# A shorter head of expert dots ahead of the second block's first half: HEAD from 26 to 12

## The reference, cut to what matters

```python
a = gelu(einsum('tpkd,td->tpk', u[idx], t))          # 128 rows of u per token
y = einsum('tpk,tpkd->td', g * a, v[idx])            # 128 rows of v per token
x = x + gt2 * y;  x = rms_norm(x, norm_f)            # end of the first block
# second block, layer 0: short convolution + memory attention, out projection, SwiGLU
# second block, layer 1: windowed attention + memory attention, out projection, SwiGLU
```

## Time and profile before

| | us |
|---|---|
| median of 3 runs | 2847.36 (2844.52 to 2847.91) |
| the profiled execution's own time | 2847.91 |
| its span | 2845.8 |
| PE busy | 2320.9 (82%) |
| DVE busy | 1931.0 (68%) |
| POOL busy | 1064.3 (37%) |
| ACT busy | 961.0 (34%) |

### The profile page before, as it was taken

How to read it: one execution, slowest core, us unless ns; L and a number is a source line. 1 busy time by engine, 2 the same in 40 slices (tenths; PEclk the granted TensorE clock), 3 DMA queues, 4 the chain that set the end, 5 groups by cost and what they waited for, 6 DMA issues and landing times.

```text
span 2845.8 us, 43889 instructions
## 1 busy us (share of the span) xinstructions
PE 2320.9 (82%) x16542; PEld 1721.4 (60%) x16542; DVE 1931.0 (68%) x4242; ACT 961.0 (34%) x1655; POOL 1064.3 (37%) x1029
## 2 busy tenths in 40 slices
PE   7998987989355555665759989869999899999998
PEld 4776776746101111111648777626788899986998
DVE  3454766799866667767997777664545676665765
ACT  4454655221100000001324333324333554455544
POOL 0000000446677777776565766576551000000000
PEclk7999999999698988988869999979999999999999
DMA  7331102879999999999989999999997345551554
GB/s 306 118 142 62 55 23 83 338 295 401 409 409 409 409 409 409 409 409 392 341 312 361 408 408 409 408 353 406 376 408 287 133 164 189 188 179 61 178 192 141
DMA packets 225234, 810.35 MB, mean 285 GB/s; under 512 B 24704, under 2 KB 30720, under 8 KB 223232
## 3 DMA queue, kind: packets, MB, share of 16 engines
q0 software_dynamic: 147456, 536.94, 48.3%
q1 hardware_dynamic: 77568, 270.61, 26.3%
HBM read 805.35 MB, written 2.10 MB: 284 GB/s over the span
## 4 chain that ended last, share of the span: by engine, by line
PE 37%; DMA 22%; DVE 14%; issue 5%; POOL 3%; ACT 1%; SPq 0%; POOLq 0%; DVEq 0%; ACTq 0%
PE ps L1844 9%; PE ps L1845 9%; PE ps L1846 9%; DMA pe_ring<-in_v,pe_vidx 7%; DVE pe_ring L2675 6%; DMA pe_ring<-in_u,pe_idx 6%; PE ps L1784 5%; DMA pe_more<-in_u,pe_idx 3%; DVE la_w_lo L2723 3%; DMA pe_more<-in_v,pe_vidx 1%; DMA la_k<-in_v,pe_vidx 1%; POOL pe_ring L1677 1%; PE ps L1739 1%; PE ps L1923 1%; PE ps L665 1%
## 5 line engine op out<-in xcount | busy, mean ns | idle before, releaser
L1844 PE MATMUL ps<-la_h_hi,la_w_hi 128*128 128x256 f32 x1856 | 531.8, 287 | 32.7 <-DVE la_w_lo L2723 25.9
L1671 POOL DMA_INDIRECT pe_ring<-in_u,pe_idx x419 | 447.8, 1069 | 287.1 <-DVE pe_dots L2675 139.1
L1784 PE MATMUL ps<-pe_ring,pe_spot 128*32 128x512 f32 x1616 | 398.7, 714 | 182.5 <-DMA pe_ring<-in_v,pe_vidx 158.5
L1846 PE MATMUL ps<-la_h_hi,la_w_lo 128*128 128x256 f32 x1856 | 524.2, 282 | 0.0
L1845 PE MATMUL ps<-la_h_lo,la_w_hi 128*128 128x256 f32 x1856 | 524.1, 282 | 0.0
L2723 DVE TENSOR_TENSOR la_w_lo<-la_w_raw,la_w_hi 128x1024 fp32r<-128x1024 f32 (+1 forms) x368 | 440.0, 1196 | 77.4 <-ACT la_w_hi L2299 76.7
L2299 ACT ACTIVATE la_w_hi<-la_w_raw 128x1024 fp32r<-128x1024 f32 (+1 forms) x368 | 379.7, 1034 | 323.5 <-DMA la_w_raw<-in_down 97.2
L1677 POOL DMA_INDIRECT pe_ring<-in_v,pe_vidx x404 | 416.7, 1032 | 175.8 <-issue 104.0
L1844 PEld LDWEIGHTS ps<-la_h_hi,la_w_hi 128*128 128x128 f32 x1856 | 355.2, 191 | 67.6 <-DVE la_w_lo L2723 42.9
L2675 DVE CUSTOM_DVE_ANT_0 pe_ring<-pe_ring,ps 128x1024 f32<-128x1024 f32 x249 | 297.9, 1219 | 117.9 <-DMA pe_ring<-in_u,pe_idx 114.4
L1845 PEld LDWEIGHTS ps<-la_h_lo,la_w_hi 128*128 128x128 f32 x1856 | 352.6, 190 | 0.4
(11 more groups left out here) (392 smaller groups left out, 3817.4 us busy)
## 6 DMA issues: line engine op xcount, KB each, us to landing
la_w_raw<-in_gate SPq DMA_DIRECT2D x88, 512.0 KB, 4.2
la_w_raw<-in_up SPq DMA_DIRECT2D x88, 512.0 KB, 4.5
la_w_raw<-in_down SPq DMA_DIRECT2D x64, 448.0 KB, 3.8
la_w_raw<-in_a_in SPq DMA_DIRECT2D x40, 512.0 KB, 5.4
wring<-in_w_in SPq DMA_DIRECT2D x32, 512.0 KB, 3.8
la_w_raw<-in_down SPq DMA_DIRECT2D x32, 512.0 KB, 3.7
wring<-in_wq SPq DMA_DIRECT2D x22, 512.0 KB, 7.3
xT<-in_w_mod_rows SPq DMA_DIRECT2D x8, 1024.0 KB, 4.9
```

The lines of the kernel that those rows point to most:

```text
L1671: pool.indirect_dma_start(row(n), None, io["u"], bass.IndirectOffsetOnAxis(idx[:, t, j:j + 1], 0)).then_inc(land[GATHERS[n][0]], 16)
L1784: return pe.matmul(ps[PER * grp:PER * grp + PER, half, :], spot[:, j // TOKENS % 2, grp, lo:lo + PER], row(n)[:, half * 512:(half + 1) * 5 ...
L1844: pe.matmul(slot(n), parts_hi[:, n % SPLIT, i, :], hi[:, k, :], start=first, stop=False)
L1846: return pe.matmul(slot(n), w_lo[:, n % RAW, i, :], hi[:, k, :], start=False, stop=last)
```

## The change

`HEAD` goes from 26 to 12. In the head on DVE, eight dots between the third low part of weights and the wait for the norm go, and six after the last `chunk_lo`; the eight dots ahead of the low parts and the four between the `scale_x` stay (with other indices).

```diff
-    EARLY, HEAD, IN_PSUM = GROUPS_U * GROUP_U, 26, 8
+    EARLY, HEAD, IN_PSUM = GROUPS_U * GROUP_U, 12, 8
...
                     for u in range(SPLIT - 1):
                         split_lo(u)
-                    for j in range(EARLY + 8, EARLY + 16):
-                        dot(2, j)
                     dve.wait_ge(rooted, rooted_at(0, -1))
                     for k in range(KC):
                         scale_x(p, k)
                         if k:
                             chunk_lo(p, 0, k - 1, ROWS_B["norm_mix"])
                         if k % 2:
-                            dot(2, EARLY + 16 + k // 2)
+                            dot(2, EARLY + 8 + k // 2)
                     chunk_lo(p, 0, KC - 1, ROWS_B["norm_mix"])
-                    for j in range(EARLY + 20, EARLY + HEAD):
-                        dot(2, j)
```

## The result

The changed kernel took 2868.8 us (median of 4 runs, 2865.5 to 2873.0) beside 2847.6 for the kernel before (4 runs, 2844.5 to 2851.1): a ratio of 1.0082 [1.0067, 1.0095]. It is slower by 21 to 23 us where +9.0 was forecast, and lies above the forecast's range. The profiled execution took 2873.6 us for a span of 2871.5; its further 4 us beside the median arise behind `half(0)`, most of them in 2521 to 2721 us, and the medians don't show them.

A forecast was written before the change was run, and what follows sets the result against it. It took `half(0)` as a relay, paced by DVE, then DMA, then PE. Terms -2.4 (to tick 38) + 7.7 + 0 + 3.7 = +9.0 us on the median 2847.4 gave 2856.4 us; 8-in-10 range 2843 to 2864.

The forecast's parts named there:

- The head: Start of `half(0)`: eight dots ahead of the scaling go, so the first product comes 9.3 us earlier.
- The reload: First reload of a weight tile, for which DVE waits 3.47 us: saves 2.3 us (0 to 3.5).
- Out projection: Layer 0, ticks 30 to 38: seven more dots on a nearly full DVE, +6.9 us (+1.6 to +8.2).
- Feed-forward and q, k, v: Ticks 38 to 118: six more gather uses where DMA sets the pace, 1.28 us each, +7.7 us.
- Last stretch: Out projection and feed-forward, ticks 158 to 226: eight more rows of v at PE's 0.46 us, +3.7 us.
- Layer 1's attention (118 to 158): Ticks 118 to 158, pace called mixed: 74 gather uses instead of 75, 0 us (-1.3 to 0).
- Rival 3: Whole debt at the DMA's price, last stretch DMA-bound: +13.5 us, 2860.9 us, up to 2866; chance 0.16.
- Rival 1: Early start survives, buffers in flight lend the gathers: -8.9 us, 2838.5 us; chance 0.14.
- the marks named for a right forecast: Included: first product at 1366.6 us, DVE idle 9 us, attention 4 to 6 us later, last gather 8 later.
- the three named for a wrong one: Below 400 GB/s in 1540 to 1840 us with PE full; attention earlier; PE awaiting v rows in last feed-forward.
- The rule beside the rows: DVE dots reading two SBUF operands slow POOL's gather issue through a shared port, 0.94 to 1.97 us.
- The price named beside the forecast: Ticks 38 to 118, if POOL at 2.27 us a gather set the pace: 13.6 us, sum +14.9.

The follow-up runs named there:

- the repeat: The changed kernel run once more, nothing altered: 1.0072, 2871.9 us.
- LAG -9: Kernel before, old head, with every gather's use due 14 earlier: 0.9972, 2845.0 us beside 2850.5.
- units of 2.0 ticks: Kernel before with an attention unit counting 2.0 ticks instead of 2.5, so fewer gathers fall there: 0.9981, 2847.2 us beside 2852.9.
- changed, LAG -9: Changed kernel with every use 14 earlier, giving the due values of the kernel before: 0.9987, 2849.0 us beside 2851.2 for the kernel before.
- changed, paid by tick 24: Changed kernel with a clock that makes up the 14 owed uses by tick 24: 1.0008 against the kernel before, 2853.4 us.
- changed, paid by tick 118: Changed kernel with a clock that pays the 14 owed uses evenly by tick 118: 1.0025, 2857.9 us beside 2850.5 for the kernel before.
- HEAD 20: Kernel before without only the six head dots behind the last `chunk_lo` (six owed): 1.0016, 2855.7 us.
- LAG 12: Kernel before, old head, with uses due seven later by the due values alone: 1.0006, 2853.4 us beside 2850.5.
- HEAD 18: Kernel before without only the eight head dots ahead of `scale_x` (eight owed): 1.0026, 2859.3 us.
- LAG 19: Kernel before, old head, with every gather's use due 14 later: 1.0084, 2875.1 us beside 2851.2.

## Why the prediction was wrong

**What held.** The head: -8.8 measured, -9.3 forecast. The reload: the whole 3.5 us saved, forecast 2.3. Out projection: +9.6 between products 24 and 32, forecast +6.9; DVE's 53 instructions there instead of 42 take 30.66 us instead of 24.86, the stage grows from 30.3 to 39.9 us, and its PE clock falls from 1.00 to 0.87. At product 32 the kernel stood at -1.1, forecast -2.4. Feed-forward and q, k, v: +9.1, forecast +7.7, at 406 GB/s. Last stretch: +2.0 to +3.0, forecast +3.7, PE full as before. Up to product 108 the sum was off by 2.7 us.

**The step that failed** is "Layer 1's attention (118 to 158). 74 uses instead of 75: 0 (-1.3 to 0)". It measured +10.5 us: 145.2 instead of 134.7, and 145.6 in the repeat. The step counted uses in a stage called "mixed" and priced their number. The number was right: between the cuts 90 rows are used in both kernels (34 dots and 56 rows of v after, 30 and 60 before), and 92 gathers stand there where 90 stood. What it left out is what sets the stage's pace. POOL's groups in that stage of the changed kernel (number, busy time, mean ns | idle time before them and what ended it):

```profile
L1677 POOL DMA_INDIRECT pe_ring<-in_v,pe_vidx x62 | 63.2, 1019 | 26.0 <-issue 17.1 <-PE ps L1784 7.8 <-DVE pe_dots L2675 1.1
L1671 POOL DMA_INDIRECT pe_ring<-in_u,pe_idx x23 | 30.8, 1338 | 15.9 <-PE ps L1784 8.4 <-issue 6.4 <-DVE pe_dots L2675 1.1
L1677 POOL DMA_INDIRECT pe_htok<-in_v,pe_vidx x4 | 3.7, 937 | 1.2 <-issue 1.2
L1671 POOL DMA_INDIRECT pe_htok<-in_u,pe_idx x3 | 3.7, 1249 | 0.9 <-issue 0.9
```

The same of the kernel before:

```profile
L1677 POOL DMA_INDIRECT pe_ring<-in_v,pe_vidx x63 | 65.8, 1045 | 19.3 <-issue 18.0 <-PE ps L1784 1.2
L1671 POOL DMA_INDIRECT pe_ring<-in_u,pe_idx x20 | 24.7, 1233 | 16.7 <-PE ps L1784 11.2 <-issue 5.5
L1677 POOL DMA_INDIRECT pe_htok<-in_v,pe_vidx x4 | 4.2, 1044 | 3.9 <-PE ps L1784 3.0 <-issue 0.9
L1671 POOL DMA_INDIRECT pe_htok<-in_u,pe_idx x3 | 2.8, 938 | 0.9 <-issue 0.9
```

They add up to the stage. After: 101.2 busy, 25.6 of gaps of 0.3 between issues, 18.4 waiting for buffers (for PE or DVE to free one): 145.2 us. Before: 97.5, 25.3 and 15.4, of which 3.6 lie ahead of the cut: 134.6. So POOL is never idle there for another reason, and of the 10.5 us 3.7 are issue (two gathers more, and each 0.02 us longer), 0.3 the gaps between issues, and 6.6 are buffers. This ledger says where POOL's time went and not which wait came first, since a wait for a buffer is a wait for PE or DVE to use a row. The longest ends 18 us into the stage, and 20 before, in the changed kernel and then in the kernel before:

```profile
1860.58 0.94 POOL L1671 DMA_INDIRECT pe_ring<-in_u,pe_idx  x1 [8.44 <-PE ps L1784]
```

```profile
1854.36 0.94 POOL L1671 DMA_INDIRECT pe_ring<-in_u,pe_idx  x1 [6.03 <-PE ps L1784]
```

From there on no wait for a buffer is over 0.4 us until 128 us into the stage (126 before): 1.4 us a gather, of which 0.94 + 0.30 is the least. In that stretch it can hardly catch up, and in it falls the late row of v above.

Is it the stock of rows in the buffers? "Ahead" is the number of gathers issued less the number used (rows of v by whole groups), at the beginning of the stage and at the start of the dot of row 104 of u for tile 3, which falls 9 to 24 us into it. One row for each run on chips of the first kind:

| kernel | uses in the stage | ahead at its start | ahead at dot 104 | attention, us | GB/s |
|---|---|---|---|---|---|
| LAG -9 | 82 | 12 | 14 | 128.4 | 387 |
| units of 2.0 ticks | 74 | 15 | 13 | 124.0 | 359 |
| before | 90 | 15 | 11 | 134.7 | 378 |
| changed, LAG -9 | 90 | 15 | 11 | 137.1 | 372 |
| changed, paid by tick 24 | 90 | 15 | 11 | 134.1 | 380 |
| changed, paid by tick 118 | 86 | 13 | 11 | 129.9 | 392 |
| HEAD 20 | 86 | 14 | 10 | 133.7 | 392 |
| LAG 12 | 91 | 14 | 8 | 134.8 | 386 |
| HEAD 18 | 87 | 13 | 8 | 139.1 | 376 |
| changed | 90 | 14 | 6 | 145.2 | 359 |
| changed, repeat | 90 | 14 | 5 | 145.6 | 357 |
| LAG 19 | 90 | 14 | 6 | 145.1 | 357 |

At dot 104 the three long stages have 5 or 6 rows ahead and all others 8 or more. But that count is taken inside the stage, in all runs but LAG -9 behind a wait of POOL for a buffer of 3.9 us or more, and is in part its outcome. At the stage's start the three have 14 rows ahead, as HEAD 20 and LAG 12 have, beside 15 in the kernel before, and at each of the six rounds of logits all twelve have 6 to 12. The number of uses doesn't separate them either: 90 take 134 to 137 us in three runs and 145 in the other three.

So what is shown is this: with 14 uses owed the stage is 10.5 us longer, three times out of three and with the old head too, and a row of v that comes late, with the attention's own matmuls behind it in PE's list, is where most of it is lost: from the third of these rounds to the fourth it is 19 us in all three and 11 before. But it is 15 in LAG 12, which loses nothing over the stage, and PE waits for rows of v in the other runs as well (5.5 us at most before and in LAG 12, 6.2 to 7.6 in the three). Why these three stages lose 10 us by them is not shown.

**Why 14 and not 7.** Seven uses owed (LAG 12) cost +1.7 us, which can't be told from nothing, six and eight owed by a shorter head 4.5 and 7.4, and fourteen 23. That is shown. Whether the cost rises steeply with the debt, or whether at 14 the rows of v fall badly between the attention's units, is not: no run holds one fixed and moves the other, and eleven owed ran on the other kind of chip alone. It stays open.

**The rivals.** Rival 3 was right in its sign and in that nearly the whole debt is paid: 14 x 1.28 = 17.9 us of DMA time against 21. Its mechanism was wrong, as the last stretch stayed PE's (188.4 of 189.0 us busy). Rival 1's statement, that the early start survives, is refuted most plainly by LAG 19, which is 10 us early at product 22 and has lost it by product 32. Of the marks named for a right forecast two failed: the attention began 8.0 us later (4 to 6 were named), and the last gather was 20.5 us later (8 named). None of the three named for a wrong one showed, so the list had no mark for a loss inside the attention.

**The rule beside the rows.** The mean issue of a gather of u into the ring in the attention rose from 1.23 to 1.34 us (20 and 23 gathers), and over all gathers there from 97.46/90 = 1.083 to 101.21/92 = 1.100, so 92 x 0.017 = 1.6 us of the 10.5. In the attention of the kernel before, 28 issues that overlapped a dot from SBUF took 1.37 us on average, and 33 beside no DVE operation 0.94. That agrees with the Trainium skill, page "SBUF — State Buffer", section "SBUF: two separate sides", on the port pair that DVE and GpSimd share; for a DVE operation with two SBUF inputs the page says so only against a GpSimd operation that reads SBUF, as a gather does for its row numbers. But it is the small part. The price named beside the forecast, 2.27 us a gather (1.97 of issue and 0.30) between ticks 38 and 118, did not come: 162 gathers took 195.60 us of issue, 1.21 each, as before, so 1.51 with the 0.30.

## What to carry to other kernels

Work that is put off is not priced by how many pieces fall into each stage by the plan, but by what paces the stage (here, for much of it, a queue with 1.4 us a piece and little reserve) and by what stands behind each piece in its engine's list. Cut both traces at the same pieces of work, count at each cut what is issued and what is used, and ask for each stage whether it can catch up: the stages that couldn't are found so, even where the reason stays open. A stock that is counted at one moment inside a stage can be the outcome of what it is meant to explain, so count it at the stage's start as well. An engine that is busy 37% over the kernel can set the pace in a part of one stage. And the experiment that separates a debt from the code that runs it up is to move the due values alone: here it also gave the fastest version (LAG -9, 0.9972).

## What was not expected of the hardware

The same kernel runs 6% longer on two of the chips (3014 to 3022 us instead of 2848 to 2853). In their eight profiles the stretch of gathers from 1200 to 1320 us reaches 341 to 366 GB/s instead of 409, at a granted PE clock of 0.71 to 0.85 instead of 0.91. Where the rate is 409 GB/s the traces repeat closely: the changed kernel's two profiled executions differ by 3.2 us in span, and at the cuts used above by no more than 0.3 us. The executions of one kernel spread further than that (HEAD 18: 2846 to 2866), and no trace here shows where.
